# Block three's local attention: heads of the two key heads in turn, score products on 64 rows, issued in twos

## The reference, cut to what matters

```python
def sliding_window_gqa(q, k, v, sinks, rel_bias):
    qb = q.reshape(B, nb, BLOCK, N_KV_HEADS, GQA_GROUP, HEAD_DIM)   # BLOCK 128, 2 key heads, 4 heads each, 64
    kb, vb = band(k), band(v)                                       # previous block | current block
    s = jnp.einsum('bnqkgd,bnskd->bnkgqs', qb, kb) * scale
    s = s + bias[None, None]
    s = jnp.where(valid, s, NEG)
    m = jnp.maximum(jnp.max(s, axis=-1, keepdims=True), sink)
    p = jnp.exp(s - m)
    p = p / (jnp.sum(p, axis=-1, keepdims=True) + jnp.exp(sink - m))
    o = jnp.einsum('bnkgqs,bnskd->bqkgd', p, vb)
```

## Time and profile before

| | |
|---|---|
| three runs | 3199.92, 3206.92, 3211.05 us; median 3206.92 |
| the profiled execution | 3207.49 us, its span 3205.7 us |
| mean granted clock over the span | 0.978 |
| PE / DVE / ACT / POOL busy over the span | 94% / 61% / 37% / 15% |
| the window attention's stretch | 2280 to 2397 us, 117 us, 3.6% of the span |

### The profile page before, as it was taken

How to read it: one execution, slowest core, us unless ns; L and a number is a source line. 1 busy time by engine, 2 the same in 40 slices (tenths; PEclk the granted TensorE clock), 3 DMA queues, 4 the chain that set the end, 5 groups by cost and what they waited for, 6 DMA issues and landing times. The chain is left out here.

```text
span 3205.7 us, 38640 instructions
## 1 busy us (share of the span) xinstructions
PE 3024.1 (94%) x14576; PEld 2431.1 (76%) x14576; DVE 1961.9 (61%) x3282; ACT 1187.2 (37%) x2227; POOL 489.9 (15%) x465
## 2 busy tenths in 40 slices
PE   7999999999899999898889989999889999999999
PEld 6787876776788888777668878745568788888887
DVE  6111744699889937829994435899875443444444
ACT  2221331477677832234356554101461211111110
POOL 1000002355111101221134143010011000000000
PEclk9999999999999999999999989999889999999999
DMA  6323125544744344241245272311001111111111
GB/s 243 141 80 111 48 83 169 174 139 132 211 106 106 119 162 169 97 107 27 80 148 184 89 230 86 119 60 49 33 11 66 66 40 53 40 53 53 53 40 66
DMA packets 190771, 324.08 MB, mean 101 GB/s; under 512 B 16434, under 2 KB 113874, under 8 KB 190586
## 3 DMA queue, kind: packets, MB, share of 16 engines
q1 hardware_dynamic: 169722, 248.72, 25.2%
q0 software_dynamic: 20864, 72.89, 6.2%
HBM read 232.14 MB, written 88.11 MB: 100 GB/s over the span
## 5 line engine op out<-in xcount | busy, mean ns | idle before, releaser
L216 PE MATMUL banks<-b3mlpw_part,b3mlp_acthi 128*128 128x512 f32 x1024 | 315.3, 389 | 0.0
L216 PE MATMUL banks<-b3h4a_hi,b3mlpw_part 128*128 128x512 f32 x960 | 298.1, 389 | 2.2 <-DVE b3mlpw_part L3949 2.2
L428 PE MATMUL banks<-b1ln_w,b_hThi 128*128 128x512 f32 x768 | 240.4, 394 | 3.3 <-DVE b_hTlo L335 3.3
L3994 DVE TENSOR_TENSOR b3out_x<-b3out_x,banks 128x1024 f32<-128x1024 f32 x128 | 154.8, 1219 | 111.6 <-PE banks L216 111.6
L216 PEld LDWEIGHTS banks<-b3mlpw_part,b3mlp_acthi 128*128 128x128 f32 x1024 | 192.2, 188 | 40.0
L3965 ACT ACTIVATE b3mlp_relu<-banks 128x1024 f32<-128x1024 f32 x32 | 32.9, 1027 | 492.6 <-PE banks L216 492.6
L216 PEld LDWEIGHTS banks<-b3h4a_hi,b3mlpw_part 128*128 128x128 f32 x960 | 179.9, 187 | 43.1 <-DVE b3mlpw_part L3949 2.6
L2358 PE MATMUL banks<-b2h_hi,b2h_whi 128*128 128x512 f32 (+1 forms) x448 | 181.6, 405 | 18.6 <-ACT b2ring_row L2386 8.4
L216 PE MATMUL banks<-b3mlpw_part,b3mlp_actlo 128*128 128x512 f32 x512 | 199.2, 389 | 0.0
L530 PE MATMUL banks<-b_hThi,b1item_hi 128*128 128x512 f32 x464 | 195.4, 421 | 3.4 <-DVE b1item_lo L519 3.1
L216 PE MATMUL banks<-b3out_lo,b3mlpw_part 128*128 128x512 f32 x480 | 189.5, 395 | 0.0
(11 more groups left out here) (501 smaller groups left out, 6937.4 us busy)
## 6 DMA issues: line engine op xcount, KB each, us to landing
qk_spill<-b1scan_qk SPq DMA_DIRECT2D x64, 256.0 KB, 3.3
b1att_k<-qk_spill SPq DMA_DIRECT2D x64, 256.0 KB, 7.5
b1out_ws<-in_w_out SPq DMA_DIRECT2D x16, 1024.0 KB, 5.0
b3mlpw_stage<-in_w_mlp_down SPq DMA_DIRECT2D x16, 1024.0 KB, 4.8
b2h_stage<-in_w_in SPq DMA_DIRECT2D x30, 512.0 KB, 4.7
b3mlpw_stage<-in_w_mlp_up SPq DMA_DIRECT2D x15, 1024.0 KB, 5.0
b1item_stage<-in_w_in SPq DMA_DIRECT2D x29, 512.0 KB, 4.0
b1ln_stage<-in_w_in SPq DMA_DIRECT2D x12, 1024.0 KB, 5.2
```

What stands on the lines that cost most here:

```text
L216: last = pe.matmul(out, x, y, start=i == 0, stop=i == n - 1)
L428: last = pe.matmul(K.bank[n % 6], a, b, start=part + k + c == 0, stop=part + k + c == 6)
L3994: v.tensor_tensor(K.m4.x3[:, st], K.m4.x3[:, st], pair, ALU.add).then_inc(S["ml_acc"], 1)
```

## The change

The two memsets and the wait for them are gone, and the zero halves of `m.qT` are not read any more. `window(u)` takes the heads in the order 0, 4, 1, 5, 2, 6, 3, 7, so that units 2j and 2j+1 are a head of key head 0 and one of key head 1. A score product now takes only the 64 partitions of its key head, rows 0 to 63 of the array for even units and rows 64 to 127 for odd ones. PE issues the two of a pair one right after the other in every even step, and none in the odd steps. Before the pair it waits once, for DVE's shift of unit r-2 (`wn_shift`, r-1), the later of the two units that had the pair's banks before.

```diff
@@ pool_gate
-    g.memset(m.qT[HD:P, :, 0], 0.0).then_inc(S["q3_edge"], 1)
-    g.memset(m.qT[0:HD, :, 1], 0.0).then_inc(S["q3_edge"], 1)
@@ act_qkv3
-    a.wait_ge(S["q3_edge"], 2)
@@ window
-    return u % NH, st, n, st + 1 - n
+    return u % NH // 2 + u % 2 * (NH // 2), st, n, st + 1 - n
@@ pe_window
-        u = r
-        if u < N:
-            h, st, n, t0 = window(u)
-            if u >= 3:
-                pe.wait_ge(*S.at("wn_shift", u - 2))
-            pe.matmul(K.bank[u % 3][:, 0:n * P], m.qT[:, h % 4, h // 4, st * P:(st + 1) * P], m.kT[:, t0 * P:(st + 1) * P], start=True, stop=True).then_inc(S["wn_sc"], 1)
+        if r < N and r % 2 == 0:
+            if r >= 2:
+                pe.wait_ge(*S.at("wn_shift", r - 1))
+            for u in (r, r + 1):
+                h, st, n, t0 = window(u)
+                g, rr = h // 4, slice(h // 4 * HD, (h // 4 + 1) * HD)
+                pe.matmul(K.bank[u % 3][:, 0:n * P], m.qT[rr, h % 4, g, st * P:(st + 1) * P], m.kT[rr, t0 * P:(st + 1) * P], start=True, stop=True).then_inc(S["wn_sc"], 1)
```

## The result

The changed kernel is slower: 3216.77 us in the median of 22 runs (3204.52 to 3223.89), against 3208.22 for the kernel before (22 runs). The ratio is 1.0022, 95% interval 1.0012 to 1.0032, some 7 us. I forecast 3206.4 and a range up to 3215; the direction and the place outside the range were both missed. Of the miss, 1.3 us is the starting point: the kernel before stood at 3206.92 us in three runs.

A forecast was written before the change was run, and what follows sets the result against it. No engine was full; the 117 us loop was taken as a relay bound by its chain of waits. Score products -1.3 us and the wait +0.8 gave -0.5, from the median 3206.92 to 3206.4 us; range 3197.5 to 3215.

The forecast's parts named there:

- The price of a pair: Score products on PE: two overlap and cost one product, 0.43 us (0.85 at the lower clock), plus array changes.
- the sum: PE's saving on score products: 0.03 us a pair at the upper clock, 0.25 at the lower, together -1.3 us.
- The change into and out of the row split: Around each pair on PE: 0.40 us for both changes at the upper clock, 0.60 at the lower.
- Rival A: Score pairs nearly free of switching because weight loads are made ahead: 3199.9 us, chance 0.16.
- rival B: The two row halves do not overlap, so pairs keep their price and pay both changes: 3213.4 us, chance 0.14.
- One sign: Within a score pair on PE: 0.22 us from the first to the second pass.
- The wait: PE's later wait for DVE's shift: about 0.1 us more DVE idling once a row, +0.8 us.
- The memsets: Removing 7.2 us of POOL work and the wait is worth 0, hidden by PE's 125 us run of products.
- the stretch's mean clock: Granted clock in the changed loop: averages 0.82, with the lower level holding for 42 us of 117.
- Rival C: PE's gaps grow and the lower clock lasts longer: two more stretches 3213.2 us, three 3216.6; chance 0.12.
- Price C: In the loop, each further 7 us stretch at the lower clock costs 3.4 us if PE bounds it.

The follow-up runs named there:

- e2: Kernel before the change with each score product on its own 64 rows, one to a step, heads in the old order: ratio 1.0163 (1.0138 to 1.0187), +52 us.
- E: Bench segment of 160 score products, only pairs on the two row halves: upper clock 3.2 us after the start, then 0.43 us a pair.
- e1: Changed kernel without the row halves: new head order, pairing and later wait kept, products on all 128 rows. Ratio to the kernel before 0.9995, median 3208.74 us.
- e3: The changed kernel measured once more beside the others on one chip: ratio to the kernel before 1.0020 (1.0006 to 1.0033).
- e6: Changed kernel with every pair of score products issued twice, the second over the first: ratio to the kernel before 1.0028, median 3217.48 us.
- e5: Changed kernel with extra full-row products nobody reads, placed where TensorE waits: ratio to the kernel before 1.0030 (1.0016 to 1.0044), 3216.99 us.
- L: Bench segment of value products and transposes with one full-row score product in every second unit, no pair: upper clock after 6.5 us.
- R: Bench segment of value products and transposes with two full-row score products in every fourth unit: upper clock within 5 us.
- H: Bench segment of 96 products of 256 columns, all on rows 0 to 63: the clock doesn't rise in 82 us.
- F: Bench segment of 96 products of 256 columns on all 128 rows, nothing else: the clock rises after 3.0 us.
- e12: Kernel before the change with an idle product of 8 columns on 32 rows ahead of every second score product: ratio 1.0035 (1.0022 to 1.0047).
- N: Bench segment as L, with a product of 8 columns on 32 rows ahead of each full-row score product: upper clock after 21.6 us.
- B: Bench segment of the changed kernel's unit: value products, transposes and a pair on the two row halves every second unit; never at the upper clock in 92 us.
- D: Bench segment as B, but both products of a pair on rows 0 to 63: never reaches the upper clock, 113 us.
- K: Bench segment of value products and transposes with one score product on a row half in each unit: never reaches the upper clock, 127 us.

## Why the prediction was wrong

**The price of a pair was right.** Forecast at the upper clock: 2.05 to 2.1 us for two units, measured 2.07, a gain of 0.03 as in the sum. At the lower: a gain of 0.25, measured 4.05 - 3.80 = 0.25. The change into and out of the row split was estimated at 0.60 us at the lower clock, and e2 shows 0.59. Overlap by rows, of which no row of before told, is as complete as by columns. Rival A (no price for the change) and rival B (no overlap) are both refuted. One sign was off: the first and second passes start 0.32 us apart and not 0.22, so half of what I had put ahead of the pair lies between its passes. In E, where no change of form comes between, it is 0.22.

**The wait was slightly mis-sized.** I gave it +0.8 us and expected DVE to wait slightly more than 13.7 us for scores. It waited 13.2 us, TensorE 2.6 us for the shift, and e1, which has the same wait, is at 0.9995. It cost nothing that can be told.

**The memsets** cost nothing by my reasoning, and nothing here contradicts it; they were not tried by themselves.

**The step that failed is the clock.** I took the stretch's mean clock as given, 0.82, and let the change act only on prices at either level. The sum has no term for it, and e1, e2 and e3 show that the row split brings one: the mean clock went from 0.83 to 0.73 and the lower clock from 41 to 65 us (71 in e3). Rival C, with 12 chances in 100, had this outcome, but by another mechanism: gaps of TensorE that grow. They shrank. Over the stretch TensorE was idle for 117.3 - 94.1 = 23 us before and for 120.2 - 100.6 = 20 us after, so the changes did fill gaps, as I had argued against C, and the clock fell all the same. I had asked only whether TensorE would have more gaps. The changed unit of the bench has none at all and stays at the lower clock, and so does the loop of e2 for 90 us.

**How well the size fits.** In the 22 runs of the changed kernel time falls as the clock rises: from about 3223 us at 0.969 to between 3204.5 and 3210.7 at 0.975 to 0.976, by fit 2.3 us for 0.001. The 97 runs of the kernel before give 2.2. A thousandth of the span's clock is 6.4 us at the lower level, so each us of it costs 0.36. For the 24 us of the two profiles that is +8.8, less the 1.3 saved on products: +7.5, against 7 by the ratio and 8.6 by the medians. This agreement is luck: the 24 us are those of a quick run, and the two profiled executions differ by only 2.8 us. By the mean clocks of all runs, 0.972 against 0.978, it is 38 us and +13 to +14, so the rest of the change would have to gain 5 to 7 us, and the sum has only 1.3. Runs at the same clock say so too: at 0.975 to 0.976 the changed kernel took 3204.5 to 3210.7 us (4 runs), the kernel before 3210.7 to 3221.2 (16 runs). Either the pairs save more than 1.3 us, or the added time at the lower clock lies where it costs less than 0.36; no run separates the two. Price C (3.4 us for 7, 0.49 for one) was higher than the fit.

That the lower clock is what costs is thus an inference, from the pair's own price (a gain at either clock), from e1 (the rest of the change costs nothing), from e6 (7 us of added work cost 0.7 to 2 when the clock rose) and from the spread of the runs; e5, made to show it directly, did not.

**What stays open:** why pairs on the two halves among value products and transposes stay low, when the same pairs by themselves (E) rise and half as many full products (L, R) do. The runs separate half rows from full rows (H and F) and from changes of form (e12, and N against B); they do not say what in the half-row product counts for less. Nor is the bench the whole loop: the changed kernel does come to the upper clock at times (its stretch has 0.73), which B never does, and what in the loop raises it was not tried. The memsets' part is open too, as said.

## What to carry to other kernels

Before halving TensorE's work, look at the granted clock of the stretch, and ask what its clock will be when those products are gone or changed in form; at a clock that changes by a factor of two this can outweigh the saving. Look at the mean clock of every run too, since one profile can be an unusual run. Splitting the array by rows pays little where a pair stands alone, since each change into and out of the split costs 0.2 us at the upper clock and 0.3 at the lower: both together are about the 0.43 us that a pair saves at the upper clock, and two thirds of the 0.85 at the lower. And try a loop's products alone in a bench: one run of 0.7 ms showed what the views of the real kernel only hinted at.

## What was not expected of the hardware

- TensorE without a gap at the lower clock: 90 us in the real loop (e2); in the bench 92 us (B), 113 us (D), 82 us (H, products on one half alone), 75 us (G, value products of 64 columns and transposes alone), 127 us (K, one half-row product a unit).
- The same half-row products at the upper clock when nothing but pairs on both halves runs (E: 160 products in 36.0 us, up after 3.2 us).
- A kernel with 32 more pairs of products (e6) only 0.7 us slower in the median (2 by the ratios), while the mean clock of its runs went from 0.972 to 0.976.
